# Two PE transposes of a recurrent and SwiGLU block become DMA transposes, and the back half of a head's step is emitted eight links later

## The reference

```python
proj = h @ w_in                                  # (B, S, 8192), split in eight
f = lb + (1 - lb) * sigmoid(f_logit); k = 1 - f; g = log(f)
q = silu(q_in) * 128 ** -0.5;  v = i_in
# HGRN2: 8 heads, state S of 128 x 128 per head, scanned forward in time
#   S_t = diag(f_t) S_{t-1} + k_t^T v_t ;  o_t = S_t^T q_t
o = rms_norm(o) * silu(o_gate);  y_a = o @ w_hg_out
u = glu_v * sigmoid(glu_g); u = causal_depthwise_conv(u)      # 31 taps
y_b = silu(layer_norm(u)) @ w_conv_out
mixed = sigmoid(gate_a) * y_a + sigmoid(gate_b) * y_b
h = layer_norm(alpha * h + mixed @ w_out)        # first norm
h = layer_norm(alpha * h + (silu(h @ w_g) * (h @ w_u)) @ w_ffn_out)
```

## Time and profile before

| | us |
|---|---|
| median of 3 runs (lowest 2385.63, highest 2552.16) | 2388.7 |
| the profiled execution, its own time | 2388.81 |
| its span, first to last instruction, slowest core (core 1) | 2387.1 |
| spans of the eight cores | 2376.2 to 2387.1 |

### The profile page before, as it was taken

How to read it: one execution, slowest core, us unless ns; L and a number is a source line. 1 busy time by engine, 2 the same in 40 slices (tenths; PEclk the granted TensorE clock), 3 DMA queues, 4 the chain that set the end, 5 groups by cost and what they waited for, 6 DMA issues and landing times.

```text
span 2387.1 us, 40618 instructions; the slowest of 8 cores (2376.2 to 2387.1 us)
## 1 busy us (share of the span) xinstructions
PE 2311.7 (97%) x14062; PEld 1161.8 (49%) x14062; DVE 1309.1 (55%) x1933; ACT 1173.4 (49%) x1682; POOL 505.0 (21%) x599
## 2 busy tenths in 40 slices
PE   7999999999999889999999999999999999999998
PEld 3555555555555543444444444444444444444443
DVE  3666665766666764555553544536364535455334
ACT  4777787888888784444442331313222232224120
POOL 4444343444343343333320000000000000000000
PEclk9999999999999999999999999999999999999999
DMA  9566373664561546343334442434334333424240
GB/s 160 94 112 99 65 125 46 108 107 65 98 93 44 138 88 147 80 116 89 95 104 129 137 141 92 165 106 150 132 126 140 124 125 120 138 86 166 76 156 36
DMA packets 95975, 263.56 MB, mean 110 GB/s; under 512 B 9920, under 2 KB 34624, under 8 KB 92224
## 3 DMA queue, kind: packets, MB, share of 16 engines
q1 hardware_dynamic: 77008, 195.69, 24.9%
q0 software_dynamic: 18768, 65.28, 18.8%
HBM read 275.88 MB, written 61.87 MB: 141 GB/s over the span
## 4 chain that ended last, share of the span: by engine, by line
PE 85%; DVE 5%; ACT 4%; issue 4%; DMA 2%; POOL 1%; DVEq 0%; ACTq 0%; SPq 0%; POOLq 0%
PE psb L417 84%; ACT L438 1%; DMA sb_y<-yD 1%; PE psb L422 1%; DVE sb_YT L486 1%; DVE sb_y L470 1%; DVE sb_Tb L470 1%; ACT sb_F L438 1%; DVE sb_y L446 1%; DMA sb_W<-w 1%; ACT sb_rso L438 1%; DVE sb_ub L470 0%; DVE sb_sab L470 0%; ACT sb_U L438 0%; DVE sb_F L627 0%
## 5 line engine op out<-in xcount | busy, mean ns | idle before, releaser
L417 PE MATMUL psb<-sb_xT,sb_W 128*128 128x512 bf16 x2560 | 740.4, 384 | 19.6 <-DMA sb_xT<-xt 5.5
L417 PE MATMUL psb<-sb_hT,sb_f1r 128*128 128x512 bf16 x2816 | 681.2, 379 | 0.0
L438 ACT ACT_TABLE_LOAD x273 | 350.3, 1283 | 296.0 <-PE psb L417 130.0
L417 PEld LDWEIGHTS psb<-sb_hT,sb_f1r 128*128 128x128 bf16 x2816 | 273.4, 98 | 325.9
L417 PE MATMUL psb<-sb_W,sb_xT 128*128 128x128 bf16 x2048 | 404.2, 221 | 5.5 <-DVE sb_vt L477 4.1
L417 PE MATMUL psb<-sb_wf,sb_actb 128*128 128x512 bf16 x1408 | 346.4, 379 | 0.4 <-DVE sb_actb L446 0.2
L417 PEld LDWEIGHTS psb<-sb_xT,sb_W 128*128 128x128 bf16 x2560 | 240.0, 98 | 186.5 <-issue 35.9
L417 PE MATMUL psb<-sb_xT,sb_wj 128*128 128x512 bf16 x1024 | 311.8, 380 | 2.8 <-DVE sb_sab L470 1.5
L446 DVE TENSOR_TENSOR sb_actb<-sb_sg,psb 128x512 bf16<-128x512 f32 x176 | 118.6, 685 | 271.7 <-PE psb L417 169.5
L438 ACT ACTIVATE sb_sg<-psb 128x512 f32<-128x512 f32 x176 | 102.7, 596 | 296.7 <-PE psb L417 294.2
L417 PEld LDWEIGHTS psb<-sb_W,sb_xT 128*128 128x128 bf16 x2048 | 195.2, 99 | 69.6 <-issue 13.4
(11 more groups left out here) (105 smaller groups left out, 2845.2 us busy)
## 6 DMA issues: line engine op xcount, KB each, us to landing
sb_f1r<-f1D SPq DMA_DIRECT2D x176, 512.0 KB, 3.8
sb_Tp<-tp POOLq DMA_DIRECT2D x32, 512.0 KB, 10.1
yD<-sb_YT SPq DMA_DIRECT2D x32, 512.0 KB, 11.0
sb_y<-yD SPq DMA_DIRECT2D x64, 256.0 KB, 3.3
sb_R<-x SPq DMA_DIRECT2D x32, 512.0 KB, 4.7
out<-sb_R SPq DMA_DIRECT2D x32, 512.0 KB, 2.7
sb_W<-w POOLq DMA_DIRECT2D x47, 256.0 KB, 5.7
f1D<-wf POOLq DMA_DIRECT2D x22, 512.0 KB, 7.1
```

The lines of the kernel that those rows point to most:

```text
L417: return P.add("pe", lambda e: e.matmul(o, lhsT=l, rhs=r, start=start, stop=stop), ks(lhsT, rhs), out.k, dur=max(60, fsz(r)) / 2400.0 + 0. ...
L438: return P.add("act", lambda e: e.activation(out=o, in_=i, func=func, **kw), rd, out.k, dur=0.19 + fsz(o) / 1200.0 + 0.09 * ptr, tbl=ACT_S ...
```

## The change

`back` no longer transposes on PE. A new helper `dmatr` lets SP issue a DMA transpose, and `front` issues one for the whole `K2[p]` right after the multiplication that writes it. `back` begins with eight empty links, then goes on with the scores as before. In `pre`, tiles 1 to 7 issue one DMA transpose per row block from `hb` into `hT`; tile 0 keeps the PE path. The planner models a DMA transpose with 0.8 us of SP and 2.5 us of latency, and leaves it out of the shared DMA rate.

```diff
+DTR_DUR = 0.8
+DTR_LAT = 2.5
@@ list_schedule
-            if op["dsem"] is not None:
+            if op["dsem"] is not None and op["nbytes"] == 0:
+                finish[i] = t_e + dur + op["lat"]
+            elif op["dsem"] is not None:
@@ build_nc
+        def dmatr(out, in_, dsem):
+
+            if dsem not in dnames:
+                dnames.append(dsem)
+            o, i = out.ap, in_.ap
+            return P.add("sp", lambda e: e.dma_start_transpose(out=o, in_=i), in_.k, out.k, dsem=dsem,
+                         dur=DTR_DUR, lat=DTR_LAT)
@@ front
             tt(K2[p].all(), kv[:, 64:192], e2.bc(2, [128, 4, 128]), ALU.mult, eng="pool")
+            dmatr(Kt[p].all(), K2[p].all().r("p b q -> p (b q)"), f"kt{p}")
             yield
@@ back
-            ps = newps()
-            psv = V(psb[ps][:].bitcast(BF16), [("ps", ps)])
-            for bb in range(4):
-                tr(V(psv.ap[:, bb * 128:bb * 128 + 128], psv.k), K2[p][bb, :])
-            cp(Kt[p].all(), V(psv.ap[:, 0:512].rearrange("p (a b) -> p a b", a=4), psv.k), eng="act")
-            relps(ps)
-            yield
+            for _ in range(8):
+                yield
             psA = newps()
@@ pre
                 yield from lnorm(r, 0, e_ln4, h_)
+                if t > 0:
+                    dmatr(hT[t % 2][:, tb * 128:tb * 128 + 128], h_.all(), f"ht{tb}")
+                    yield
+                    continue
                 ps = newps()
```

## The result

The changed kernel takes 2431.5 us (median of 5 runs, 2429.6 to 2432.9) against 2388.7. It is slower by 43 us where I forecast 25 us less. The ratio is 1.0174, 95% interval 1.013 to 1.0219: slower, but whether by more than 2% is left open.

The account below looks back on a forecast made before the run. The prediction took PE, busy 97% of the span, as the bound in both changed stages. From 2388.8 us it took 26.8 for slots and 2.0 for waits, added 4, and got 2364.0 us, range 2345 to 2410.

Parts of the forecast that it names:

- Slots, -26.8 us: PE time freed by removing 480 transposes at 0.056 us: 14.3 us in the first stage, 12.5 us in the third.
- hb hidden, price 0: Third stage: the DMA transposes of `hb` cost nothing, since `hT` is first read 38 us after the last `hb` block.
- L: First stage: time from the end of the `K2` multiplication to `Kt` being readable; put at 3 to 11 us, taken as 5.
- 1 us for late keys: First stage: price of PE waiting for `Kt`, at a landing time of 5 us in the newly planned order.
- Gaps past 8 us: First stage: the links push most gaps between `K2` and its first `Kt` matmul, median 6.5 us, past 8 us.
- +3 us for order and state chain: First stage: cost of the links' delay at the recurrence's end and of a state chain starting later against `vt`: 3 us.
- Doubling for the clock: Any price made of PE stalls of a us and over is doubled, because the granted clock drops after idle stretches.
- Rival B: First stage: keys come late, transposes standing on SP behind `onD` and `yD`; 110 us of stalls, 2470 us; chance 0.15.
- milder case: First stage: late keys with a landing time of 8 us, 38 us of stalls doubled, giving 2436 us.
- D: Third stage: turning 256 KB occupies SP or the DMA engines over 17 us, `f1r` late; 2472 or 2416 us; chance 0.06.
- E: First stage also tightens: less ScalarE work and a bank less take away 15 us of waits; 2344 us; chance 0.09.
- C: First stage bound by its chain: freed slots fill with waiting, only 12.5 us come back; 2376 us; chance 0.12.

## Why the prediction was wrong, point by point

- *Slots, -26.8 us.* Right: 480 matmuls less, and 12.5 us back in the third stage, to the tenth. The 14.3 us of the first stage rest on the count and the slot; no run measures them alone.
- *hb hidden, price 0.* Right, and shown by `hb` alone at 0.9946.
- *L, "take 5, near the transfer of the same size".* The step that failed, and with it the price of 1 us for late keys, measured at 80.9. In quiet L is 2.0 us to the last packet and some 2.4 to the semaphore, better than my lower bound of 3; in the nine steps under the casting loads it is 8.5 to 27, past my upper bound of 11 in seven of them. I took medians of transfers and one L for all steps. The loss is made by nine steps in the tail. One thing could have been read before: in its first 60 us the kernel before keeps the DMA engines 0.98 busy, and a store of the same 128 KB takes 11.9 us there, not the median 2.3. The number of packets, 544 against 143, needed a trace of a transpose.
- *"Gaps past 8 us" by the eight links.* Wrong. The median gap went from 6.5 to 7.6, and it is 7.6 without the links too. That `psA` and `psK` take banks late did not hold `psK` back. In the nine steps with L over 8 the gap is the landing, plus 0.1 to 0.3 us.
- *+3 us for order and state chain.* Mis-sized and of changing sign: the links alone are +17 us, and with a planned latency of 8 they save 50.
- *Doubling for the clock.* Too much. Time at 1.2 GHz grew from 21 to 93 us, but lies mostly on the waits; 4 us of the 56 are left to it, 10 at most. The doubled price of the earlier trace rows was read from waits of a us between busy stretches.
- *Rival B* had the place and the sign. One of its reasons, transposes that stand on SP behind `yD`, is seen in steps 15 and 22; the casting loads, under which all nine steps fall, it did not name. Its price of 110 us at L = 10 came from "most steps"; measured are 81 us in 11. Its turning point, 28.8 us of stalls, was exceeded. I gave it 0.15 and laid the range to 2410, while its milder case stood at 2436. The 1309 ns of the Trainium skill for one block ("VectorE: DVE Perf Modes", "The three transpose paths") would be an estimate of 5.2 us for four; all four landed in 2.3 us from the issue where nothing else was in the queues.
- *D* did not occur: no wait for `f1r` in the third stage. The 14 us fewer other waits in the changed kernel look like *E*, but they stand beside late keys. With `Kt` in time (latency 8, steps 0 to 3 on PE) *C* comes out instead: the other waits grow by 18 us, the slots of the first stage do not come back, and its start of the third stage, 1357.8, is even 9 us later than before. So with L put right the change would still not have reached 2364 in any order tried.

## What to carry to other kernels

Price a DMA on the critical path in packets for each DMA engine and by what the other queues do at that moment, and read the slowest landing, not the median. A transfer in 256 byte pieces beside a bulk load takes one large packet's time per small one, so a transfer of 128 KB that lands in 2.3 us in quiet takes 28.8. And look at what stands in front of it on its own queue. Moving a latency off the tensor engine pays where a stage has slack of tens of us (`hb`, 38 us); where the fixed order came for the result within some 8 us it didn't, and the orders planned here for a longer latency gave back as small waits what the slots had gained. The best kernel here moves `hb` alone: 2374.8 us, 0.5% under the kernel before.

## What the runs showed of the hardware

- A DMA transpose of 128x512 bf16 from SP: 1.2 us of SP, 2.3 us from issue to landing in quiet, 544 packets in the window of one; a plain copy in 256 byte runs is as slow in traffic (29.2 against 28.8 us).
- Where a queue of 256 byte packets meets the busy casting queue, both move the same number of packets: 464 and 463 in 20 us.
- A 128x1024 transpose keeps SP hardly longer than the half sized one: 1229 ns in the median against the 1193 above. The view of the tile `sb_hT`:

```profile
L516 SPq DMA_TRANSPOSE sb_hT<-sb_hb x28: 1227/1229/1462, 1441.9 to 2265.2; - x28
...
DMA to landing us min/median/max: 2.8/4.2/7.0
```
